# Scattering the results of the last two experts of each layer by column half

## The reference, cut to what matters

```python
def expert_choice_moe(h, w_router, b_router, w_gate, w_up, w_down):
    b, n, d = h.shape
    cap = CAP_FACTOR * n // N_EXPERTS
    aff = jax.nn.softmax((h @ w_router + b_router).astype(jnp.float32), axis=-1)
    vals, idx = lax.top_k(jnp.swapaxes(aff, 1, 2), cap)
    xg = jax.vmap(lambda xb, ib: xb[ib])(h, idx)
    hh = jax.nn.silu(jnp.einsum('becd,edf->becf', xg, w_gate)) * jnp.einsum('becd,edf->becf', xg, w_up)
    out = jnp.einsum('becf,efd->becd', hh, w_down) * vals[..., None].astype(h.dtype)
    return jax.vmap(lambda ib, ob: jnp.zeros((n, d), ob.dtype).at[ib.reshape(-1)].add(ob.reshape(-1, d)))(idx, out)

def trunk_layer(x, cond, P, l, ctx):
    ...
    x = x + g1 * (merged @ P['w_out'][l])
    h2 = rmsnorm(x, P['norm2_g'][l]) * (1 + sc2) + sh2
    x = x + g2 * expert_choice_moe(h2, P['w_router'][l], P['b_router'][l], P['w_gate'][l], P['w_up'][l], P['w_down'][l])
    return x, new
```

## Time and profile before

| | us |
|---|---|
| median of 3 runs | 2463.26 (2462.96 to 2471.12) |
| the profiled execution | 2466.59 |
| its span, first to last instruction | 2464.8 |
| TensorE busy (matmuls) | 2273.8 (92%) |
| VectorE busy | 1650.0 (67%) |
| ScalarE busy | 1200.0 (49%) |
| GpSimd busy | 257.6 (10%) |

### The profile page before, as it was taken

One profiled execution on the slowest core, in us unless ns is written; L12 is line 12 of the kernel. 1 busy time (PEld: TensorE's weight loads), 2 busy tenths in 40 slices (PEclk: granted clock), 3 DMA queues, 4 the chain that ended last, 5 costly groups with the idle time before them and its releaser, 6 DMA issues.

```text
span 2464.8 us, 36755 instructions
## 1 busy us (share of the span) xinstructions
PE 2273.8 (92%) x14193; PEld 1736.7 (70%) x14193; DVE 1650.0 (67%) x1935; ACT 1200.0 (49%) x1340; POOL 257.6 (10%) x240
## 2 busy tenths in 40 slices
PE   5999899999699999999959999999994999999997
PEld 3878778899466666666658877888992666666664
DVE  3258455435688888889843674553457888889886
ACT  4234323222367777677642432332224677777774
POOL 1102000001101111011001200000010110111101
PEclk7999999999799999999979999999996999999999
DMA  8461011125899999999945410012445999999996
GB/s 302 171 231 58 18 61 35 61 75 191 279 358 365 373 373 380 373 373 376 350 144 189 157 54 29 33 35 77 163 155 176 334 376 378 373 374 374 380 377 207
DMA packets 271387, 566.05 MB, mean 230 GB/s; under 512 B 10568, under 2 KB 12680, under 8 KB 271216
## 3 DMA queue, kind: packets, MB, share of 16 engines
q1 hardware_dynamic: 254848, 509.64, 57.4%
q0 software_dynamic: 14512, 48.05, 6.5%
q10 hardware_dynamic: 1904, 6.62, 0.8%
HBM read 542.71 MB, written 24.18 MB: 230 GB/s over the span
## 4 chain that ended last, share of the span: by engine, by line
PE 54%; DMA 9%; DVE 4%; issue 3%; ACT 2%; POOL 0%; DVEq 0%; SPq 0%; ACTq 0%; POOLq 0%
PE ps L1057 31%; PE ps L754 13%; DMA ring<-in_w_down 5%; DMA ring<-in_w_up 3%; PE ps L915 3%; DVE w_lo L1789 2%; ACT w_hi L1372 2%; PE ps L840 1%; PE ps L891 1%; PE ps L1047 1%; PE ps L701 1%; PE ps L874 1%; PE ps L715 1%; DMA ring<-in_w_gate 0%; PE ps L985 0%
## 5 line engine op out<-in xcount | busy, mean ns | idle before, releaser
L1789 DVE TENSOR_TENSOR w_lo<-ring,w_hi 128x2048 fp32r<-128x2048 f32 x384 | 877.8, 2287 | 133.3 <-ACT w_hi L1372 130.9
L1372 ACT ACTIVATE w_hi<-ring 128x2048 fp32r<-128x2048 f32 x384 | 736.8, 1920 | 310.4 <-PE ps L1057 196.6
L1057 PE MATMUL ps<-w_hi,xT 128*80 128x512 f32 x2112 | 669.2, 395 | 5.1 <-DVE EP L1804 2.9
L754 PE MATMUL ps<-WH,HTH 128*128 128x256 f32 x1840 | 535.4, 291 | 7.4 <-DVE ringL L1475 3.5
L754 PE MATMUL ps<-ringL,HTH 128*128 128x256 f32 x1840 | 517.0, 281 | 0.0
L754 PE MATMUL ps<-WH,HTL 128*128 128x256 f32 x1840 | 516.4, 281 | 0.0
L1057 PEld LDWEIGHTS ps<-w_hi,xT 128*80 128x80 f32 x2112 | 315.3, 149 | 181.7 <-issue 8.0
L1057 PE MATMUL ps<-w_lo,xT 128*80 128x512 f32 x1056 | 418.3, 396 | 0.0
L754 PEld LDWEIGHTS ps<-WH,HTH 128*128 128x128 f32 x1840 | 348.2, 189 | 35.4 <-issue 26.5
L754 PEld LDWEIGHTS ps<-ringL,HTH 128*128 128x128 f32 x1840 | 348.6, 189 | 0.8
L754 PEld LDWEIGHTS ps<-WH,HTL 128*128 128x128 f32 x1840 | 347.6, 189 | 0.0
(11 more groups left out here) (196 smaller groups left out, 2070.9 us busy)
## 6 DMA issues: line engine op xcount, KB each, us to landing
ring<-in_w_gate SPq DMA_DIRECT2D x128, 1024.0 KB, 11.7
ring<-in_w_up SPq DMA_DIRECT2D x128, 1024.0 KB, 11.6
ring<-in_w_down SPq DMA_DIRECT2D x128, 1024.0 KB, 12.7
ring<-in_w_mod SPq DMA_DIRECT2D x23, 2048.0 KB, 8.0
ring<-in_w_in SPq DMA_DIRECT2D x18, 2048.0 KB, 7.9
ring<-in_w_out SPq DMA_DIRECT2D x4, 2048.0 KB, 9.1
ring<-in_w_o SPq DMA_DIRECT2D x4, 1536.0 KB, 6.3
Y<-x_save POOLq DMA_DIRECT2D x10, 512.0 KB, 7.2
```

What stands on the lines that cost most here:

```text
L754: last = nc.tensor.matmul(dst, a[:, t, k], w, start=k == 0 and i == 0, stop=k == KB - 1 and i == 2)
L1057: last = nc.tensor.matmul(ps[0:CE, bank], lhs[:, a, kb], w[:, u, k], start=kb == 0 and i == 0, stop=kb == KB - 1 and i == 2)
L1372: nc.scalar.activation(w_hi[:, u % UB], ring[:, raw[0], 4 * (u % 2):4 * (u % 2) + 4], ACT.Copy).then_inc(hi_ready, 1)
L1789: TT(w_lo[:, u % UB], ring[:, raw[0], 4 * (u % 2):4 * (u % 2) + 4], w_hi[:, u % UB].bitcast(f32), ALU.subtract).then_inc(lo_ready, 1)
```

## The change

The loop of whole-row scatters now covers experts 0 to 13. The last two experts are sent by column half: `scatter_half(e, h)` waits for one half of the expert (`out_evac[h]`) and for the half scatter of the same columns before it (`eo_half[h]`, one semaphore for each side), and sends 80 rows of 512 columns (2 KB). The halves of 14 also wait for the scatter of 13. The target is seen as 1280 rows of 512 columns, so the halves need indices of their own, 2 x row + h, which VectorE writes into `idx2` in four more instructions. ScalarE, before it loads x, and GpSimd, at the end of the layer, wait on the two new semaphores. Counts of `eo_saved` are adapted (14 a layer instead of 16).

```diff
+        idx2 = sb("idx2", [128, 2, E], u32)
...
+        idx2_ready = sem("idx2_ready")
+        eo_half = [sem(f"eo_half{h}") for h in range(2)]
...
                     if l or e:
-                        pool.wait_ge(eo_saved, 16 * (l * E + e))
+                        pool.wait_ge(eo_saved, 16 * (l * (E - 2) + e))
...
+                def scatter_half(e, h):
+
+                    pool.wait_ge(out_evac[h], l * E + e + 1)
+                    pool.wait_ge(eo_half[h], 16 * (2 * l + e - E + 2))
+                    settle(pool, 2)
+                    pool.indirect_dma_start(x_out[l].rearrange("r (h c) -> (r h) c", h=2),
+                                            bass.IndirectOffsetOnAxis(ap=idx2[0:CE, h, e:e + 1], axis=0),
+                                            eo[0:CE, e % 2, 512 * h:512 * h + 512], None, compute_op=ALU.add
+                                            ).then_inc(eo_half[h], 16)
...
-                    scatter(e)
-                pool.wait_ge(eo_saved, 16 * E * (l + 1))
+                    if e < E - 2:
+                        scatter(e)
+                        continue
+                    if e == E - 2:
+                        pool.wait_ge(idx2_ready, 2 * (l + 1))
+                        pool.wait_ge(eo_saved, 16 * (E - 2) * (l + 1))
+                    for h in range(2):
+                        scatter_half(e, h)
+                for h in range(2):
+                    pool.wait_ge(eo_half[h], 32 * (l + 1))
...
-                    act.wait_ge(eo_saved, 16 * E * l)
+                    act.wait_ge(eo_saved, 16 * (E - 2) * l)
+                    for h in range(2):
+                        act.wait_ge(eo_half[h], 32 * l)
...
+                for h in range(2):
+                    TS(idx2[0:CS, h], slotT[0:CS, 0, 0:E], 2.0, float(h), ALU.mult, ALU.add)
+                    TS(idx2[CS:CE, h], slotT[CS:CE, 0, 32:48], 2.0, 1024.0 + h, ALU.mult, ALU.add).then_inc(idx2_ready, 1)
...
-                        dve.wait_ge(eo_saved, l * (16 * E) + (16 * e - 16))
+                        dve.wait_ge(eo_saved, l * (16 * E - 32) + (16 * e - 16))
```

## The result

The changed kernel is slower: 2480.6 us (median of 6, 2478.72 to 2481.73) beside 2463.95 (6 runs, 2462.51 to 2471.12), a ratio of 1.0062 (95% interval 1.005 to 1.0074). The prediction, 2460.5 with a range up to 2466.0, was wrong, and not by a term of its sum: the time is lost where the change touches no instruction.

What follows compares the result with a forecast made beforehand. TensorE holds 54% of the span; the change pays only where TensorE stands still behind a scatter. Layer 0's -1.9 and layer 1's -0.9 make -2.8 us, from the median 2463.26 to 2460.5; range 2457.5 to 2466.0.

Steps and rivals of the forecast that it cites:

- No case comes near 12 us: Whole kernel: no case reaches the 0.5%, 12.3 us, that the measurement can tell from no change; within 0.5% 0.96.
- The last issue of layer 0 comes 0.98 us sooner: Gap after layer 0: right 15 waits only for its weighing, issued at 1235.41; bounds 0.1 later and 0.98 sooner.
- rival (b): Layer 0's gap: right 14 lands as late as the whole, holding right 15 to 1236.4; -1.8, 2461.5; chance 0.12.
- rival (c): Layer 0's gap: GpSimd becomes the bound, left 14 over 11.1 us or left 15 2.69; 2464.5 to 2465.9; chance 0.09.
- the bound by bytes: GpSimd's time on a scatter: if by bytes instead of rows, 0.7 us more saved at each of two ends.
- A half lands 0.9 sooner: Last scatter of each layer: a half saves 0.9 us from issue to landing against a whole; bounds 0 and 1.3.
- Rival (a): Last landing of each layer: a half lands no sooner than a whole, only 0.98 left, 2462.3; chance 0.22.
- More waits: Before layer 1 and at the end: GpSimd and ScalarE wait on two or three semaphores instead of one; cost nothing.
- A landing that is earlier by d starts layer 1 by d sooner: Gap between the layers: loads of x and squares hang on the last landing, so its whole gain reaches layer 1.
- 20 to 21: Gap between the layers: TensorE's idling in us expected after the change, against 22.38 before.
- Index arithmetic at nothing: Four VectorE instructions a layer, 0.7 us, covered by VectorE's 5.81 us idling and SP's slack; 1.4 in all if uncovered.
- The sum: Whole kernel: -1.9 in layer 0 and -0.9 in layer 1, -2.8 us; forecast 2460.5, chance 0.52.

Runs made afterwards that it cites:

- x1: Kernel before with 128 unused bytes a partition where the change allocates idx2, no instruction differing; 2478.8 us, ratio 1.0055.
- x2: Changed kernel with idx2 moved behind all other buffers, so every buffer lies where it lay before; 2467.92 us, ratio 1.0011.
- z1: Changed kernel with idx2 allocated at 256 bytes a partition, half of it unused; 2470.07 us, ratio 1.0008.
- z3: Changed kernel with idx2 at 256 bytes and its four index instructions moved behind the first two subtractions; 2464.63 us, ratio 0.9992.
- z2: Kernel before with idx2 at 256 bytes and the four index instructions of each layer only, scatters whole; 2467.31 us, ratio 1.0007.
- y1: Kernel before with 128 unused bytes directly ahead of HTH, small and expert buffers staying in place; 2478.96 us, ratio 1.0051.

## Why the prediction was wrong, step by step

**"No case comes near 12 us": the step that failed.** The argument went through the instructions that the change adds and moves, and took 1,270 us of mixers as untouched since none of them is in the diff. The one line of the diff that reaches them is the allocation, and no rival held it. With x1 that line alone, without any of the others, is 13.6 us (0.0055 of 2465). Why the place matters stays open.

**The last issue of layer 0 comes 0.98 us sooner: wrong.** GpSimd in the gap of the kernel after:

```profile
1228.01 2.60 POOL L688 DMA_INDIRECT x_save<-EP,idx  x1 [25.89 <-issue]
1230.92 2.56 POOL L688 DMA_INDIRECT x_save<-EP,idx  x1 [0.31 <-issue]
1234.89 1.40 POOL L688 DMA_INDIRECT x_save<-EP,idx  x1 [1.41 <-DMA x_save<-EP,idx]
1241.22 1.40 POOL L688 DMA_INDIRECT x_save<-EP,idx  x1 [4.93 <-DMA x_save<-EP,idx]
```

Left 15 went at 1234.89, well before the last weighing at 1238.75, as forecast. The last one went 2.51 us after the last matmul (1238.71), before 2.55, and was released by a DMA: rival (b). Right 14, issued at 1230.92, had landed at 1240.45 (0.77 ahead of that issue), 9.5 us later, beside a weight load, as the whole one had with 9.5 (9.6 in the prediction). In the three versions without the shift it was the place of rival (c). x2:

```profile
1220.93 5.46 POOL L689 DMA_INDIRECT x_save<-EP,idx  x1 [26.22 <-issue]
1226.69 1.40 POOL L689 DMA_INDIRECT x_save<-EP,idx  x1 [0.30 <-issue]
1232.97 1.40 POOL L689 DMA_INDIRECT x_save<-EP,idx  x1 [4.87 <-DVE EP L1831]
1234.67 1.40 POOL L689 DMA_INDIRECT x_save<-EP,idx  x1 [0.30 <-issue]
```

The first half occupies GpSimd for 5.46 us where I had put 2.69, and takes long to land (x2, issues from 1220 to 1221: count, median us to landing):

```profile
x_save<-EP,idx POOLq DMA_INDIRECT x1, 11.3
```

That is past the 11.1 that (c) names. Left 15 starts 0.77 after this landing (1232.20), which is what it waits for; the weighing in its brackets raises the other half's semaphore. Right 15 goes when left 15 is off GpSimd, 3.04 after the last matmul (z1 3.12, z3 3.22). So the bound by bytes is out: while VectorE rests, the issue of a half takes 1.40, as that of a whole does. Rows, 80 in both, fit that. What the prediction had wrong is how long VectorE can hold an issue up. x2's VectorE at that time:

```profile
1219.98 2.28 DVE L1816 TENSOR_TENSOR w_lo<-ring,w_hi 128x2048 fp32r<-128x2048 f32 x1
1222.17 0.74 DVE L1831 SCALAR_TENSOR_TENSOR EP<-ps,colv,g2bc 80x512 f32<-80x512 f32 x1
1222.84 2.28 DVE L1816 TENSOR_TENSOR w_lo<-ring,w_hi 128x2048 fp32r<-128x2048 f32 x1
```

The issue ends at 1226.39, 1.27 after the second subtraction (1225.12). In the kernel after the two long ones end at 1230.61 and 1233.48, again 1.27 and 1.28 after a subtraction (1227.06 + 2.28 and 1229.92 + 2.28):

```profile
1227.06 2.28 DVE L1815 TENSOR_TENSOR w_lo<-ring,w_hi 128x2048 fp32r<-128x2048 f32 x1
1229.92 2.28 DVE L1815 TENSOR_TENSOR w_lo<-ring,w_hi 128x2048 fp32r<-128x2048 f32 x1
```

An issue that meets no subtraction takes 1.40. It looks as if GpSimd gets on only once a subtraction is over. The Trainium skill (GPSIMD Engine Reference, "1. Specifications") says that GpSimd shares its SBUF interfaces with VectorE and contends with VectorE's instructions that have two SBUF inputs; `w_lo` is one, and these rows agree. Which subtraction an issue gets past they don't tell: left 14 starts 0.95 us into the first of two subtractions both here and in x2, with the same 0.58 between the two, and is done after the first here (2.60) and after the second in x2 (5.46). It is the second in both layers of x2, z1 and z3 and in layer 1 of the changed kernel; why not in its layer 0 stays open.

**A half lands 0.9 sooner: nearly right, and the end's 0.9 is in part luck.** The last halves of the changed kernel (issues from 1241 to 1242 and from 2463 to 2464):

```profile
x_save<-EP,idx POOLq DMA_INDIRECT x1, 3.9
...
out<-EP,idx POOLq DMA_INDIRECT x1, 3.9
```

That is 1.1 and 1.2 less than the 5.0 and 5.1 before. From the last issue of layer 0 to the loads of x it is 5.02 us before and 4.03 after (1241.22 to 1245.25 below); 3.96, 3.99 and 3.93 in x2, z1 and z3. At the end, from the last issue to the end of the span, 14.26 before (2450.54 to 2464.8) and 13.36 after:

```profile
2451.23 5.44 POOL L688 DMA_INDIRECT out<-EP,idx  x1 [26.20 <-issue]
2463.44 1.39 POOL L688 DMA_INDIRECT out<-EP,idx  x1 [2.22 <-DVE EP L1830]
```

Rival (a) is out. From the last issue to the loads of x the eleven other kernels with whole scatters took 4.95 to 5.24, so a half is about 1 us sooner; the 0.4 estimated from the Trainium skill's formula (DMA: Bandwidth & Descriptors, "Anatomy of one DMA") is refuted for these scatters. The last issue of layer 1 still hangs on its weighing, as forecast, though the first half held GpSimd for 5.44 us here too: there was time for it. **The end gains 0.87 to 0.9, as predicted**, but as the difference of two terms: the landing is 1.2 sooner, and from it to the end of the span it is 9.55 us in all four kernels with halves where it is 9.16 in the twelve with whole scatters. GpSimd's first load after layer 0's last landing, too, starts 0.60 after it (1245.15 to 1245.75) and not 0.29 (1241.39 to 1241.68). What both places share is the second semaphore that GpSimd waits for, which the prediction priced at nothing under *More waits*; no run takes that wait apart.

**A landing that is earlier by d starts layer 1 by d sooner: only in part.** After, the loads of x were issued 1.03 sooner after the last matmul than before (6.54 against 7.57), and the gap shrank by 0.26. ScalarE in the gap:

```profile
1245.25 2.35 ACTq L1160 DMA_DIRECT2D X<-x_save  x5
1251.26 1.04 ACT L1149 ACTIVATE QK<-X 128x1024 f32<-128x1024 f32 x1
1254.03 1.06 ACT L1149 ACTIVATE QK<-X 128x1024 f32<-128x1024 f32 x1 [0.40 <-ACT QK L1149]
1255.62 1.06 ACT L1149 ACTIVATE QK<-X 128x1024 f32<-128x1024 f32 x1 [0.43 <-DMA X<-x_save]
1257.07 1.06 ACT L1149 ACTIVATE QK<-X 128x1024 f32<-128x1024 f32 x1 [0.31 <-DMA X<-x_save]
```

The last two squares now wait 0.43 and 0.31 us for the tiles of x. Those tiles landed 9.0 and 10.0 us after their issue, before 7.7 and 8.5, when each was there 0.7 ahead of its square. The third square stands idle for 0.40 although its tile had landed at 1253.23; it does so in x2, z1 and z3 as well, and no row gives a reason. With these three, issue to first matmul grew by 0.77 (14.81 to 15.58). So the loads' own time changed, which the prediction had left as it was. In x2, z1 and z3 the loads came 0.4 to 0.6 sooner after the last matmul than before, only the third square's wait is there, and the gap was 21.94, 22.12 and 22.21 against 22.07 to 22.65 in the twelve kernels with whole scatters: 0.1 to 0.4 below the mean of these, and two of the three inside their range. I had predicted 20 to 21.

**Index arithmetic at nothing: wrong.** I had looked for cover on VectorE and at SP, and found it. The price is on GpSimd, by the mechanism above: the first gather's issue ends 0.85 us after the first subtraction, which now comes 0.65 later. z2 shows 2.88 and 2.94 us for the first gathers of the two layers, before 2.23 and 2.28, so +0.65 each. In the changed kernel itself layer 1 paid it (2.97), and layer 0 happened to have its gather through ahead of the subtraction (0.98). z3 takes it away in layer 1 (2.28); its 0.98 in layer 0 is no work of the edit, since y1, without any index instruction, has it too.

**The sum** that the runs put in place of -2.8: the gap -0.1 to -0.4, the end -0.9, the gathers up to +1.3, so about 0 without the shift. x2 and z1 bear that out: the lower ends of their intervals are -0.7 and -1.2 us, so -2.8 is out for them. For z3, without the gathers' price, the same sum is -1.0 to -1.3, and its interval, -4.2 to +0.5, can't tell this from nothing or from -2.8. The shift comes on top, 12.6 us (y1's ratio) to 15.3 (the mixers of the changed kernel).

## What to carry to other kernels

A new buffer can change the time of every instruction that reads a buffer behind it: put it behind the others, or compare the addresses of the matmul operands before and after, and time the padding alone before any story about the edit is believed. Before an indirect DMA is cut in two on GpSimd, look at what VectorE does at that moment: here the issue of a half took 1.40, 2.60 or 5.46 us by the subtractions it met, with the same bytes and rows. And a wait that is shortened gives its gain only as far as what follows keeps its own time: here later loads and an idling square behind it took back 0.77 of 1.03 us.

## What the hardware showed that I had not expected

- The pace of matmuls on stationary fp32r tiles of 128 x 128 depends on where that buffer lies against others: 2.83 us for 24 of them or 2.88, nothing in between in most kernels; 64 and 128 bytes more are slow, 192 and 256 fast, and 128 bytes more for all buffers together are fast. The expert matmuls, 395 ns each before and after, show nothing of it.
- An indirect scatter's issue on GpSimd takes 1.40 us alone and, for expert 14, where it meets a subtraction of VectorE, ends 1.27 or 1.28 us after one of them: 2.56 to 2.70 in all where it is the first that it meets, 5.43 to 5.46 where it is the second of two.
